# Scores of the HGRN rounds in three groups over three PSUM banks instead of four groups over two

## The reference, cut to what matters

```
S_t = diag(f_t) S_{t-1} + k_t i_t^T,   o_t = S_t^T q_t

diff   = cum[t] - cum[s]                       # cumulated log f
decay  = where(s <= t, exp(min(diff, 0)), 0)
scores = einsum('bhtsk,bhsk->bhts', q[t] * decay, k[s])
o      = o_inter + einsum('bhts,bhsv->bhtv', scores, v)
```

## Time and profile before

| | |
|---|---|
| median of 3 runs | 921.77 us (921.39 to 922.09) |
| profiled execution, its own time | 921.26 us |
| its span, first to last instruction | 919.5 us |
| PE busy | 908.8 us, 99% of the span |
| DVE, ACT, POOL busy | 527.5, 368.4, 235.3 us |
| mean granted TensorE clock | 0.995 of full speed |
| the four rounds of section B | about 115 to 252 us, 34.2 us each |

### The profile page before, as it was taken

One profiled execution on the slowest core, in us unless ns is written; L12 is line 12 of the kernel. 1 busy time (PEld: TensorE's weight loads), 2 busy tenths in 40 slices (PEclk: granted clock), 3 DMA queues, 4 the chain that ended last, 5 costly groups with the idle time before them and its releaser, 6 DMA issues.

```text
span 919.5 us, 21173 instructions
## 1 busy us (share of the span) xinstructions
PE 908.8 (99%) x8080; PEld 897.4 (98%) x8080; DVE 527.5 (57%) x635; ACT 368.4 (40%) x506; POOL 235.3 (26%) x289
## 2 busy tenths in 40 slices
PE   9999999999999999999999999999999999999995
PEld 9999999999999999999999999999999999999995
DVE  6432278787765566665576666666666433435654
ACT  7223446646454565223353333333333222213433
POOL 0006087687111100004621111111111121213441
PEclk9999999999999999999999999999999999999998
DMA  7332534233255443633323333333333333332312
GB/s 227 105 93 84 180 93 104 57 94 100 61 135 147 127 122 109 199 119 100 92 70 93 92 91 91 91 91 91 91 91 108 96 94 94 94 93 69 105 34 94
DMA packets 176474, 94.75 MB, mean 103 GB/s; under 512 B 17889, under 2 KB 174961, under 8 KB 176017
## 3 DMA queue, kind: packets, MB, share of 16 engines
q1 hardware_dynamic: 149698, 80.61, 29.5%
q10 hardware_dynamic: 26736, 13.60, 5.5%
HBM read 86.25 MB, written 8.03 MB: 103 GB/s over the span
## 4 chain that ended last, share of the span: by engine, by line
PE 98%; DVE 1%; DMA 0%; ACT 0%; ACTq 0%; issue 0%; DVEq 0%
PE acc L496 87%; PE lvb L634 1%; PE lvb L496 1%; PE lvb L527 1%; PE mb L742 0%; PE mb L695 0%; PE ob L670 0%; PE lvb L630 0%; PE acc L508 0%; PE mb L725 0%; PE ob L721 0%; PE lvb L706 0%; PE ob L720 0%; PE ob L665 0%; PE lvb L580 0%; PE mb L683 0%
## 5 line engine op out<-in xcount | busy, mean ns | idle before, releaser
L886 ACT ACTIVATE whi<-raw 128x1024 fp32r<-128x1024 f32 (+2 forms) x132 | 146.8, 1112 | 366.5 <-PE acc L496 365.8
L1247 DVE TENSOR_TENSOR wlo<-raw,whi 128x1024 fp32r<-128x1024 f32 (+2 forms) x131 | 197.5, 1508 | 155.7 <-ACT whi L886 155.7
L496 PE MATMUL acc<-xah,whi 128*128 128x260 f32 x896 | 185.5, 288 | 0.0
L496 PE MATMUL acc<-xah,wlo 128*128 128x260 f32 x896 | 180.3, 283 | 0.0
L496 PE MATMUL acc<-xal,whi 128*128 128x260 f32 x896 | 179.9, 282 | 0.0
L496 PE MATMUL acc<-xbh,whi 128*128 128x260 f32 x816 | 165.0, 283 | 0.0
L496 PE MATMUL acc<-xbh,wlo 128*128 128x260 f32 x816 | 164.4, 283 | 0.0
L496 PE MATMUL acc<-xbl,whi 128*128 128x260 f32 x816 | 164.2, 283 | 0.0
L496 PEld LDWEIGHTS acc<-xah,whi 128*128 128x128 f32 x896 | 137.9, 188 | 1.8
L496 PEld LDWEIGHTS acc<-xal,whi 128*128 128x128 f32 x896 | 137.9, 188 | 0.0
L496 PEld LDWEIGHTS acc<-xah,wlo 128*128 128x128 f32 x896 | 137.9, 188 | 0.0
(11 more groups left out here) (302 smaller groups left out, 1165.2 us busy)
## 6 DMA issues: line engine op xcount, KB each, us to landing
raw<-in_w_in SPq DMA_DIRECT2D x96, 256.0 KB, 3.1
raw<-in_w_up SPq DMA_DIRECT2D x88, 256.0 KB, 3.1
raw<-in_w_down SPq DMA_DIRECT2D x16, 384.0 KB, 3.3
raw<-in_w_down SPq DMA_DIRECT2D x16, 320.0 KB, 3.7
raw<-in_w_out SPq DMA_DIRECT2D x16, 256.0 KB, 3.1
raw<-in_w_ple_gate SPq DMA_DIRECT2D x8, 512.0 KB, 3.6
x_transposed<-xstg SPq DMA_DIRECT2D x1, 2080.0 KB, 7.6
hT<-x_transposed ACTq DMA_DIRECT2D x1, 2080.0 KB, 9.0
```

Of the source, the lines that this page charges most:

```text
L496: mm = pe.matmul(sums[:, b, 0:HT], wt[slot][:, w], xx[:, c, b * HT:(b + 1) * HT], start=first and i == 0 and q == 0, stop=last and i == n ...
L886: act.activation(whi[k % 2][:, 0:n], raw[k % 2][:, 0:n], ACT.Copy).then_inc(hi_ready, 1)
L1247: dve.tensor_tensor(wlo[k % 2][:, 0:n], raw[k % 2][:, 0:n], whi[k % 2][:, 0:n].bitcast(fp), SUB).then_inc(lo_ready, 1)
```

## The change

The levels are computed in three groups: 0 to 2, 3 to 5, and 6 with the sums for the diagonal. Level l goes to bank l % 3 of three, the third being `mb`; the sums for the diagonal stay in bank 1 of `lvb`. On TensorE the order becomes

```diff
+        def score_bank(l):
+            return (lvb[:, 0, :], lvb[:, 1, :], mb[:])[l % 3]
...
-                levels = [l for l in (2 * use, 2 * use + 1) if l < LV]
+                levels = [l for l in range(3 * use, 3 * use + 3) if l < LV]
                 pe.wait_ge(zq_ready, it * LV + (levels[-1] + 1))
-                pe.wait_ge(merged, it * MERGES + (2 * use + 1))
-                taken()
-                if use == 3:
+                pe.wait_ge(merged, it * MERGES + (3 * use + 1))
+                taken()
+                if use == 0:
+
+                    wait_misc(M_B, 0, it, 4)
+                if use == 2:
...
-                        out = lvb[:, l % 2, c * 128:(c + 1) * 128].rearrange("s (two t) -> s two t", two=2)
+                        out = score_bank(l)[:, c * 128:(c + 1) * 128].rearrange("s (two t) -> s two t", two=2)
...
                 halves(0, it, first_scores)
-                scores(1, it)
-                halves(1, it, lambda: scores(2, it))
-                scores(3, it)
+                halves(1, it, lambda: scores(1, it))
+                scores(2, it)
                 pe.wait_ge(prep, it * 8 + 8)
-                wait_misc(M_B, 0, it, 4)
...
# ScalarE
                     ahead("B", k, it)
+                    if k == 0:
+                        pad_queries(5, it)
                     act.wait_ge(rot_done, it * 2 + (k + 1))
...
-                        for l in range(5, LV):
-                            pad_queries(l, it)
+                        pad_queries(6, it)
...
# VectorE
-                for n in (2 * use, 2 * use + 1):
+                for n in range(3 * use, min(3 * use + 3, LV + 1)):
...
-                    src = lvb[:, n % 2, :].rearrange("s (e b h) -> s e b h", e=8, h=hb)
+                    src = score_bank(n).rearrange("s (e b h) -> s e b h", e=8, h=hb)
...
                     last_gate(before)
-                merge(1, it)
                 done("B", 0, it)
                 ahead("B", 0, it)
+                merge(1, it)
...
                 rotate(qr[:, it, :], 0, it)
-                merge(2, it)
...
-                merge(3, it)
+                merge(2, it)
                 rotate(kr[:, it, :], 1, it)
```

## The result

The changed kernel takes 923.03 us (median of 20 runs, 922.64 to 924.85), the kernel before 921.72 us (median of 20 runs). The forecast was 922.8 us, +1.04 us.

What follows compares the result with a forecast made beforehand. TensorE, busy 908.8 of 919.5 us, was taken to bound the kernel. A 2.40 us stall minus a 1.36 us saving gave +1.04 us, 922.8 us on the median; the 8-in-10 range was 921.0 to 924.2 us.

Steps and rivals of the forecast that it cites:

- Part 1: TensorE's groups of scores: four become three, saving two borders, 0.34 us a round, 1.36 us in all.
- Part 2: P1a, second product on TensorE, waits for `last_gate` behind the added merge: 0.80 us in rounds two to four, 2.40 us.
- Part 3: Other waits of TensorE at the groups of scores and for the levels, all costed at nothing, with each one's cover.
- S0 for `misc_free`: First group of scores waits for `misc_free`: costed at nothing, cover 0.1 to 0.2 us, upper bound 0.2 us a round.
- S1 for level 5: Second group of scores waits for GpSimd's padded level 5: costed at nothing, cover at least 0.8 us.
- S2 and the levels: Third group waits for merges of levels 3 to 5, cover 1 us; levels 6 and 7 ready before needed; costed at nothing.
- The sum: Whole kernel: stall 2.40 minus saving 1.36 gives +1.04 us, 922.8 us on the median, +0.11%.
- the signs I had named: Profile after: three gate waits about 0.7 us, level 2 merge 0.71, later rounds 0.4 to 0.5 longer, first 0.3 shorter.
- No stall at all: Rival at P1a: stall absent or smaller than the gain, result -1.36, 920.4 us; chance 0.1.
- The slow third merge: Rival at VectorE's merge(0): third merge takes 1.33 us, 0.62 more in three rounds, +2.9, 924.7 us; chance 0.08.
- S0's wait: Rival at the first group: waits for `misc_free` 0.1 to 0.3 us in three rounds, +1.3 to +1.9 us; chance 0.15.
- The clock: Rival on TensorE: stalls halve its clock for half a product, 2.89 us three times, 8.7, 931 us; chance 0.02.

Runs made afterwards that it cites:

- e3: Kernel e1 with level 2 as a group of its own between the first and second product, four groups again: 922.38 us, ratio 1.0005 to the kernel before.
- e8: Kernel e7 with the first instruction of the rotation of q ahead of the second group's merges on VectorE: 920.00 us, ratio 0.9985 to the kernel before.
- e1: Changed kernel with the last gate ahead of the merge of level 2, behind those of levels 0 and 1: 920.72 us, ratio 0.9989 to the kernel before.
- e7: Changed kernel with the last gate ahead of all merges of its round on VectorE: 920.51 us, ratio 0.9989 to the kernel before.
- e6: Changed kernel with the last gate later still on VectorE, behind the low weights of the third product: 935.58 us, ratio 1.0149 to the kernel before.
- e2: Kernel before with only the third bank and the first group's wait for `misc_free`, still four groups: 921.58 us, ratio 1.0000.
- e4: Kernel e7 with ScalarE's padding of level 5 back behind the crosswise copies of rq: 922.75 us, ratio 1.0017 to the kernel before.

## Why the prediction was right, and which terms were off

- **Part 1, one group fewer saves 0.34 us a round.** Right. A group's borders cost 0.32 us in e3's chain, and e8, which has no named wait left, gains 1.45 us in the median against 1.36, and 1.23 in the stretch, 0.31 a round. The rule of the Trainium skill, "TensorEngine Tiling (Array Packing)", section "Key Properties", that a change of tiling mode drains TensorE, agrees in direction; that a drain is what is paid here no run shows, and the price is this trace's.
- **Part 2, P1a waits for `last_gate`.** The step that decided the sign, and right in place, number and cause: three waits, none in the first round, gone in e1 and e7, larger in e6. The size was off. I had P1a at 5.21 us after S0, it came at 5.42. Of the 0.21 us, 0.13 are a later end of the gate (5.28 for 5.15: it overlaps the merge before it by 0.1 instead of 0.2, and takes 0.75), and 0.08 the signal (0.14 for the 0.06 of the earlier trace rows; at the head squares of e7 it is 0.05 too, and why the first matmul of a product takes longer no run shows). In the chain the pair P0b and P1a goes from 5.96 us in the first round to about 6.9, so 0.95 us a stall against 0.80, in all 2.85 against 2.40.
- **Part 3, waits at nothing.** S0 for `misc_free`: right (e2). S1 for level 5: right, though e4 shows a thinner cover than the 0.8 us I had: 1.2 us of copies in front of the padding leave a wait of 0.6, so that 0.6 was there; the rest is the 0.24 us from the padding to the matmul. S2 and the levels: no wait in any run. Missed was the far end of VectorE's list. I followed the rotation of q only to `acc[0]`, over 2 us early, and not on to the copies of rk, which wait for it, and from there to the head squares, where in the kernel before the state update ends only 0.15 us ahead of the matmul. In the first round of the changed kernel, which has no stall, this costs 0.15 us (L687 takes 1.06 us, before 0.91), in the second and third 0.03 and 0.02, 0.2 in all. That is the larger part of why the first round is only 0.1 us shorter and not 0.34.
- **The sum.** 2.85 - 1.36 + 0.2 = +1.7 us, against +1.8 in the stretch (130.12 - 128.32), +1.5 in the spans and +1.3 (0.9 to 2.0) in the medians. Forecast +1.04. That the medians come so near to it owes a little to luck: both terms that were off pull the same way, and by the trace the forecast was 0.7 to 0.8 us short. Of the signs I had named, the wait and the merge came as told; rounds two and three grew by 0.6 to 0.7 us and not by 0.4 to 0.5, and the first shrank by 0.1 and not by 0.3.
- **The rivals.** No stall at all: that is e1, and it is what the change would have given with the gate elsewhere. The slow third merge: it takes 0.72 us. S0's wait: none. The clock: 1.00 in all four rounds.

## What to carry to other kernels

Where one engine is busy 99% of the time, look for the cost of its own switches (here 0.3 us for going from weights of 128 columns to a group with 64 and back) before looking for waits; then ask of every instruction that the regrouping pushes back who waits for it, and who waits for them, round to the end of the loop. Of a stall and a saving that nearly even out, the stall is often one short instruction in the wrong place: put the one that frees the accumulator first. A wait of 0.1 us can hide between pipelined records with no idle time to its name; compare the length of each piece of the chain with its shortest instance, and lengthen the suspected delay until it has a name.

## What the runs showed of the hardware

- TensorE kept a granted clock of 1.00 over idle times of 0.7 us (changed kernel) and fell to its lower level (0.50 from 156.8 to 162.3 us, matmuls every 0.217 us instead of 0.12) after one of 3.25 us (e6). What lies between these two lengths no run shows. I had not expected the price of a wait to jump so: three waits longer by 2.5 us each cost 12.5 us instead of 7.4.
- From the end of a VectorE instruction to the first matmul that waited for it there were 0.05 us at the head squares (e7) and 0.14 us at the start of a product (changed kernel); from the end of ScalarE's padding to the first matmul of S1 0.24 us (e4).
